# Turning softmax probabilities by a DMA transpose of sixteen-bit planes instead of by TensorE, in a hybrid attention block

## The reference, cut to what matters

```python
s = jnp.einsum('bcqhd,bckhd->bhcqk', qc, kb).astype(jnp.float32) * (Dh ** -0.5) + bias[None]
s = jnp.where(valid[None, None, :, None, :], s, -jnp.inf)
p = jax.nn.softmax(s, axis=-1).astype(v.dtype)
o = jnp.einsum('bhcqk,bckhd->bcqhd', p, vb)
...
ya = out_a.reshape(B, T, D_A) * jax.nn.silu(ga)
x = x + jnp.einsum('bte,ed->btd', y, w_out[l])
```

## Time and profile before

| | |
|---|---|
| median of 3 runs | 528.12 us (527.5 to 530.15) |
| profiled execution, span from first to last instruction | 526.3 us; the page gives no other time for it |
| PE busy | 517.4 us, 2912 matmuls |
| PEld busy | 453.4 us |
| DVE busy | 366.6 us |
| ACT busy | 273.4 us |
| POOL busy | 31.0 us |
| granted TensorE clock, mean | 0.998 of full speed |
| bytes by DMA | 102.53 MB, 195 GB/s in the mean |

### The profile page before, as it was taken

The page is one execution under the profiler, slowest core; times in us unless marked ns, Lnnn a source line. Parts: engine busy times, 40 slices in busy tenths (PEclk is TensorE's granted clock), DMA queues, the critical chain, the costliest instruction groups (busy, mean ns, idle before and its releaser), DMA issues.

```text
span 526.3 us, 8274 instructions
## 1 busy us (share of the span) xinstructions
PE 517.4 (98%) x2912; PEld 453.4 (86%) x2912; DVE 366.6 (70%) x552; ACT 273.4 (52%) x403; POOL 31.0 (6%) x47
## 2 busy tenths in 40 slices
PE   8999999999999999999999999999999999999994
PEld 6989999888888888888888888888888888888883
DVE  4799776675756787868666767586877887646454
ACT  4786555454444444445464737365555566434342
POOL 1000054040500000000000000000000000000000
PEclk9999999999999999999999999999999999999999
DMA  7975798766675566663755554645546775566614
GB/s 245 340 263 164 236 263 277 214 175 199 208 246 177 176 202 201 176 199 110 236 159 165 157 178 152 193 155 168 165 156 186 251 242 178 183 202 185 208 45 159
DMA packets 75356, 102.53 MB, mean 195 GB/s; under 512 B 5536, under 2 KB 63808, under 8 KB 75072
## 3 DMA queue, kind: packets, MB, share of 16 engines
q1 hardware_dynamic: 73744, 96.68, 58.1%
q0 software_dynamic: 1296, 5.01, 3.0%
q10 hardware_dynamic: 288, 0.46, 0.3%
HBM read 99.24 MB, written 2.11 MB: 193 GB/s over the span
## 4 chain that ended last, share of the span: by engine, by line
PE 97%; DMA 1%; DVE 0%; ACT 0%; issue 0%; DVEq 0%; POOLq 0%
PE acc L456 39%; PE acc L460 19%; PE acc L425 8%; PE acc L426 8%; PE acc L427 8%; PE acc L476 4%; PE acc L484 3%; PE aux L486 2%; DMA gain<-norm_gain 1%; PE aux L601 1%; PE aux L622 1%; PE aux L627 0%; PE aux L629 0%; PE aux L598 0%; PE aux L599 0%; PE aux L597 0%
## 5 line engine op out<-in xcount | busy, mean ns | idle before, releaser
L456 PE MATMUL acc<-acts,hi_slots 128*128 128x512 f32 (+1 forms) x896 | 276.9, 390 | 0.0
L984 DVE TENSOR_TENSOR lo_slots<-raw_slots,hi_slots 128x1024 fp32r<-128x1024 f32 x166 | 205.0, 1241 | 100.0 <-ACT hi_slots L690 99.1
L690 ACT ACTIVATE hi_slots<-raw_slots 128x1024 fp32r<-128x1024 f32 x166 | 175.1, 1057 | 149.3 <-PE acc L460 86.5
L460 PEld LDWEIGHTS acc<-acts,lo_slots 128*128 128x128 f32 x896 | 167.4, 188 | 34.0
L460 PE MATMUL acc<-acts,lo_slots 128*128 128x256 f32 (+1 forms) x896 | 174.2, 276 | 0.0
L456 PEld LDWEIGHTS acc<-acts,hi_slots 128*128 128x128 f32 x896 | 136.5, 189 | 0.1
L425 PE MATMUL acc<-hi_slots,acts 128*128 128x512 f32 x192 | 74.7, 389 | 0.0
L426 PE MATMUL acc<-lo_slots,acts 128*128 128x512 f32 x192 | 74.7, 389 | 0.0
L427 PE MATMUL acc<-hi_slots,acts 128*128 128x512 f32 x192 | 74.7, 389 | 0.0
L427 PEld LDWEIGHTS acc<-hi_slots,acts 128*128 128x128 f32 x192 | 36.0, 188 | 7.6
L425 PEld LDWEIGHTS acc<-hi_slots,acts 128*128 128x128 f32 x192 | 36.0, 188 | 7.5
(11 more groups left out here) (180 smaller groups left out, 458.1 us busy)
## 6 DMA issues: line engine op xcount, KB each, us to landing
raw_slots<-w_blocks SPq DMA_DIRECT2D x140, 512.0 KB, 4.2
raw_slots<-wo_blocks SPq DMA_DIRECT2D x32, 512.0 KB, 4.2
raw_slots<-w_blocks SPq DMA_DIRECT2D x8, 256.0 KB, 5.7
qk<-x POOLq DMA_DIRECT2D x1, 2048.0 KB, 10.2
qk<-xT SPq DMA_DIRECT2D x7, 256.0 KB, 6.6
o<-ext_dram POOLq DMA_DIRECT2D x1, 1024.0 KB, 8.1
fgain<-final_gain POOLq DMA_DIRECT2D x1, 1024.0 KB, 7.7
out<-o SPq DMA_DIRECT2D x2, 512.0 KB, 3.0
```

Source lines behind the costliest of these rows:

```text
L456: nc.tensor.matmul(whole, w_hi4[:, u % RING, q, f * HD:f * HD + HD], acts[:, k, :, tokens], start=(k == 0), stop=False)
L460: last = nc.tensor.matmul(acc[:, bank:bank + n], w_lo4[:, u % RING, q, f * HD:f * HD + HD], a_hi[:, k, tokens], start=False, stop=(k == KT ...
L690: nc.scalar.activation(hi_slots[:, s, 0:UK * CB], w_raw[:, s, :], ACT.Copy).then_inc(hi_done, 1)
L984: nc.vector.tensor_tensor(lo_slots[:, s, 0:UK * CB], w_raw[:, s, :], hi_slots[:, s, 0:UK * CB].bitcast(f32), ALU.subtract).then_inc(lo_don ...
```

## The change

The probabilities of a pair are put into one tensor `probs` (early and late side by side) and turned by one DMA. An f32 word is taken as two sixteen-bit halves. ACT copies the 768 words of a partition as 2 x 768 sixteen-bit integers into two planes (`planes_out`); SP issues one transposing DMA of the 12 blocks of 128x128 sixteen-bit elements, from SBUF to SBUF (`turn_planes`); ACT joins the turned planes to f32 words in `probs_T` (`pT_out`), and after that copies the high part pT_hi from there; DVE's low part is taken from there as well. The planes lie in `qiT`, which is free by then. The six transposes of PE and the two copies from PSUM to SBUF go; the semaphores of aux1 and aux2 that guarded them go too.

On SP the transpose of pair i stands in block i + 11 between the loads of units 1 and 2, behind a wait for the planes (for pair 7 between the loads of units 1 and 2 of the first output block). The value products of pair i move from block i + 10, before unit 7, to the next block, behind unit 0. `planes_out` stands on ACT behind the first features_low, pT_out behind stage_q, pT_rest behind DVE's stage_rest, `output` behind split 12, and for pair 7 output and gated move behind split 4 of the first output block.

```diff
+        probs_T = sb("probs_T", [P, 2, P + T])
+        probs = sb("probs", [P, 2, P + T])
+        p0, p1 = probs[:, :, 0:P], probs[:, :, P:P + T]
+        pT0, pT1 = probs_T[:, :, 0:T], probs_T[:, :, T:T + P]
...
+        WORDS = 2 * (P + T)
+        planes = flat(qiT[:, :, :]).bitcast(u16)[:, 0:2 * WORDS].rearrange("p (s n) -> p s n", s=2)
+        planes_T = flat(qiT[:, :, :]).bitcast(u16)[:, 2 * WORDS:4 * WORDS].rearrange("p (s n) -> p s n", s=2)
+
+        def halves(words):
+            return flat(words[:, :, :]).bitcast(u16).rearrange("p (n s) -> p s n", s=2)
...
+            def turn_planes(pair):
+                sp.wait_ge(planes_made, pair + 1)
+                sp.dma_start_transpose(flat(planes_T).rearrange("p (t q) -> p t q", q=P),
+                                       flat(planes)).then_inc(planes_turned, 16)
+
+            def feature_block(g, row, turned=None):
                 for u in range(UNITS):
+                    if u == 2 and turned is not None:
+                        turn_planes(turned)
                     sp.wait_ge(lo_done, g * UNITS + (u - RING + 1))
...
             def score_pair(pair, k_chunk):
...
-                pe.wait_ge(aux_read[1], pair + AUX1_PAIRS)
+                pe.wait_ge(aux_read[1], AUX1_PAIRS)
+                if pair > 0:
+                    pe.wait_ge(biased, pair)
...
             def value_pair(pair):
-                pe.wait_ge(aux_read[1], pair + (AUX1_PAIRS + 1))
-                pe.wait_ge(aux_read[2], pair + (AUX23_PAIRS + 1))
-                pe.wait_ge(aux_read[3], pair + AUX23_PAIRS)
+                pe.wait_ge(pt_lo_done, pair + 1)
+                pe.wait_ge(aux_read[3], pair + AUX3_PAIRS)
...
                 feature_unit(g, 0)
+                if pair > 0:
+                    value_pair(pair - 1)
                 feature_unit(g, 1)
...
-                feature_unit(g, 4)
-                feature_unit(g, 5)
-                transpose_pair(pair)
-                feature_unit(g, 6)
-                value_pair(pair)
-                feature_unit(g, 7)
+                for u in range(4, UNITS):
+                    feature_unit(g, u)
...
                 unit(G_OUT, u)
+                if u == 0:
+                    value_pair(HEADS - 1)
...
+            def planes_out(pair):
+
+                act.wait_ge(normed, pair + 1)
+                nc.scalar.activation(planes, halves(probs), ACT.Copy).then_inc(planes_made, 1)
+
             def pT_out(pair):
-                act.wait_ge(pt_done, pair + 1)
-                nc.scalar.activation(pT_hi, aux[2][:, :], ACT.Copy).then_inc(pt_hi_done, 1)
-                nc.scalar.activation(flat(pT1[:, :, :]), aux[1][:, 0:2 * P], ACT.Copy).then_inc(aux_read[1], 1)
+                act.wait_ge(planes_turned, 16 * pair + 16)
+                nc.scalar.activation(halves(probs_T), planes_T, ACT.Copy).then_inc(words_made, 1)
+                act.wait_ge(words_made, pair + 1)
+                nc.scalar.activation(pT_hi.rearrange("p (h t) -> p h t", h=2), pT0,
+                                     ACT.Copy).then_inc(pt_hi_done, 1)
...
                 features_low(g, 0, 0)
+                planes_out(i)
                 split_hi(g, 7)
                 split_hi(g, 8)
-                pT_out(i)
                 split_hi(g, 9)
                 stage_q(q_next, k_next, keys)
+                pT_out(i)
                 split_hi(g, 10)
-                output(i)
                 features_low(g, 1, 0)
                 split_hi(g, 11)
                 split_hi(g, 12)
+                output(i)
                 split_hi(g, 13)
...
             y_hi(1)
-            output(7)
             y_hi(2)
...
             split_hi(G_OUT, 4)
+            output(7)
             split_hi(G_OUT, 5)
...
             def pT_rest(pair):
                 dve.wait_ge(pt_hi_done, pair + 1)
-                nc.vector.tensor_tensor(pT_lo, aux[2][:, :], pT_hi.bitcast(f32),
-                                        ALU.subtract).then_inc(aux_read[2], 1)
+                hi, lo = (t.rearrange("p (h t) -> p h t", h=2) for t in (pT_hi, pT_lo))
+                nc.vector.tensor_tensor(lo, pT0, hi.bitcast(f32), ALU.subtract).then_inc(pt_lo_done, 1)
...
-            gated(3, 1)
             y_lo(6)
             split_lo(G_OUT, 4)
+            gated(3, 1)
             split_lo(G_OUT, 5)
```

More of the change, by code:

```diff
@@ L60, in hybrid_block @@
     f32r = mybir.dt.float32r
+    u16 = mybir.dt.uint16
     ALU = mybir.AluOpType
@@ L100, in hybrid_block @@
         low = sb("low", [P, 2, 2, T])
-        ki_bd = sb("ki_bd", [P, 2, T])
-        ki_nat = sb("ki_nat", [P, TM, P])
+        probs_T = sb("probs_T", [P, 2, P + T])
+        probs_T_flat = probs_T[:, :, :].rearrange("p h t -> p (h t)")
+        ki_bd = probs_T_flat[:, 0:2 * T].rearrange("p (h t) -> p h t", h=2)
+        ki_nat = probs_T_flat[:, 2 * T:3 * T].rearrange("p (m t) -> p m t", m=TM)
         w_idx1 = sb("w_idx1", [P, IDX_H])
@@ L123, in hybrid_block @@
         ones = sb("ones", [P, 1])
-        p1 = sb("p1", [P, 2, T])
-        p0 = sb("p0", [P, 2, P])
-        pT1 = sb("pT1", [P, 2, P])
+        probs = sb("probs", [P, 2, P + T])
+        p0, p1 = probs[:, :, 0:P], probs[:, :, P:P + T]
+        pT0, pT1 = probs_T[:, :, 0:T], probs_T[:, :, T:T + P]
         neg_max = sb("neg_max", [P, 2, 2])
@@ L221, in hybrid_block @@
         normed = sem("normed")
-        pt_done = sem("pt_done")
+        planes_made = sem("planes_made")
+        planes_turned = sem("planes_turned")
+        words_made = sem("words_made")
         pt_hi_done = sem("pt_hi_done")
+        pt_lo_done = sem("pt_lo_done")
         pv_done = sem("pv_done")
@@ L245, in hybrid_block @@
         AUX1_INDEX, AUX1_PAIRS = 1, 5
-        AUX23_PAIRS = 1
+        AUX3_PAIRS = 1
         HALF = CHUNK
@@ L354, in _, with out_unit @@
             token_block(G_VA, ROW_VA)
-            with sp.Fori(G_QKA, G_OUT) as g:
-                feature_block(g, g)
-            with sp.Fori(G_OUT, G_END) as g:
+            feature_block(G_QKA, G_QKA)
+            for g in range(G_QKA + 1, G_OUT):
+                feature_block(g, g, g - (G_QKA + 1))
+            def out_unit(g, u):
+                sp.wait_ge(lo_done, g * UNITS + (u - RING + 1))
+                load(u, wo_blocks[ds(g - G_OUT, 1), u, :, :].rearrange("o p c -> (o p) c"))
+            for u in range(2):
+                out_unit(G_OUT, u)
+            turn_planes(HEADS - 1)
+            for u in range(2, UNITS):
+                out_unit(G_OUT, u)
+            with sp.Fori(G_OUT + 1, G_END) as g:
                 for u in range(UNITS):
-                    sp.wait_ge(lo_done, g * UNITS + (u - RING + 1))
-                    load(u, wo_blocks[ds(g - G_OUT, 1), u, :, :].rearrange("o p c -> (o p) c"))
+                    out_unit(g, u)
             for n, (m, c) in enumerate(VECTOR_PARTS):
@@ L897, in gate_block @@
                 features_low(g, 0, 0)
+                planes_out(i + 4)
                 split_hi(g, 7)
@@ L900, in gate_block @@
                 split_hi(g, 8)
-                pT_out(i + 4)
                 split_hi(g, 9)
@@ L904, in gate_block @@
                     stage_q(q_next, q_next + 4, 8)
+                pT_out(i + 4)
                 split_hi(g, 10)
@@ L909, in _ @@
                 gate_block(g, i, i + 1)
-                output(i + 4)
                 features_low(g, 1, 0)
@@ L914, in _ @@
                 tanh_gate(i, 1)
+                output(i + 4)
                 split_hi(g, 13)
@@ L1353, in feature_attention @@
                 split_lo(g, 8)
-                pT_rest(i)
                 split_lo(g, 9)
                 stage_rest(q_next, k_next, i + 1)
+                pT_rest(i)
                 split_lo(g, 10)
@@ L1380, in gated @@
                 dve.wait_ge(gate_rated, 2 * i + (half + 1))
-                dve.wait_ge(aux_read[3], 2 * i + (half + AUX23_PAIRS + 1))
+                dve.wait_ge(aux_read[3], 2 * i + (half + AUX3_PAIRS + 1))
                 nc.vector.tensor_tensor(y, y, z[:, half, :], ALU.mult).then_inc(gate_step, 1)
@@ L1395, in gate_block @@
                 split_lo(g, 8)
-                pT_rest(i + 4)
                 split_lo(g, 9)
@@ L1399, in gate_block @@
                     stage_rest(i + 1, i + 5, i + 5)
+                pT_rest(i + 4)
                 split_lo(g, 10)
```

1 line of the change is left out of this document (removed).

## The result

| | before | after |
|---|---|---|
| median of 5 runs each | 528.37 us (527.5 to 530.15) | 524.25 us (524.02 to 525.87) |
| ratio | | 0.9936, 95% interval 0.9921 to 0.995 |
| span of the profiled execution | 526.3 us | 523.8 us |

The forecast was 524.5 us. The change takes 4.1 us off. The sum of the forecast came out right, but two of its terms were off in opposite directions, as the profile after shows.

What follows compares the result with a forecast made beforehand. PE, busy 98% of the 526.3 us span, was taken as the bound: less 5.3 us of transposes, plus a 1.7 us wait, plus 1.8 us from span to median gave 524.5 us; whole range 522.7 to 540.

Steps and rivals of the forecast that it cites:

- Removed, 5.3 us: 48 transposes leave PE in the attention blocks, 0.66 us for each of 8 pairs, a gain of at most 5.3 us.
- Added on ACT: Parting and joining passes at 1.5 us each, net 21 us in all on ACT, hidden if in time.
- D: Time from the planes being made to the transposing DMA's landing, taken as 5.5 us.
- Deadlines of pairs 0 to 6: PE waits before value products only if D exceeds 7.8 us, or 8.65 in pairs 4 to 6.
- Pair 7, wait of D - 3.8, at least 0.7: PE's wait for y_lo(0) before the first output unit, 1.7 us with D of 5.5.
- Sum: Span 526.3 - 5.3 + 1.7 = 522.7, plus 1.8 to reach the median: 524.5 us.
- B: Rival: DMA runs piece by piece, D is 9.1, PE waits at every value product: 534.7 us, chance 0.2.
- C: Rival: serial DMA stretches, D is 14.4, weights late too: 577.1 us, chance 0.1.
- A: Rival: gain eaten by D of 6.4 to 8.6, or half-rate ACT passes with D of 5: 526.2 us, chance 0.2.
- the formula: Span as 521.0 + (D - 3.8) + 4 (D - 7.8) + 3 (D - 8.65), positive brackets only, first at least 0.7.
- break-even: The D at which PE's waits cancel the whole gain, put at 8.1 us.
- The page against the change: Trainium skill page: 390 ns on TensorE against 1309 ns by DMA; twelve blocks in turn would make D 15.7 us.

Runs made afterwards that it cites:

- E1: Kernel after, with the six transposes of each pair put back on PE between units 5 and 6, into a bank nobody reads: 528.67 us, 1.0014 of before.
- E2: Kernel after, with pair 7's join and high and low parts moved behind y_hi(0), y_hi(1) on ACT and y_lo(0), y_lo(1) on DVE: 522.52 us, 0.9894 of before.
- E6: Kernel after, with the joining pass walking word by word, writing without a stride and reading the two planes in turn: 523.63 us, 0.9906 of before.
- E3: Kernel after, with the transpose done twice in series, the second issued when the first has landed: 533.69 us, 1.0104 of before.
- E8: Kernel after, with each pair's transpose issued as twelve DMAs of one 128x128 block each: 619.74 us, 95.5 us more than after.
- E4: Kernel after, with value products back in the pair's own block before unit 7: 552.9 us in the quicker two executions (1.0468 of before), 562.11 and 562.4 in the others.
- E5: Kernel after, with the transpose done three times in series, each issued when the one before has landed: 572.28 us.
- E7: Kernel after, with pair 7's join moved behind y_hi(0) and y_hi(1) and the joining pass walking word by word: 522.7 us, 0.9886 of before.

## Why the prediction was right, step by step

- **Removed, 5.3 us:** right. E1 takes 4.4 back, plus the 0.7 that the last wait absorbs; E2 shows 5.2 gained once nothing waits.
- **Added on ACT:** the parting pass was priced at 1.5 us and takes 1.47; the joining pass was priced the same and takes 1.94. Busy time grew by 23.7 us, not 21. The step "1.5 us each, because element count sets the f32 rows" failed for the joining pass; E6 shows that the order of its reads and writes is part of its price.
- **D, 5.5 us:** wrong by 1.75; it is 3.75. The count of pieces was right, 1,536 (and 32 packets more), but a quarter of the way towards 66 ns a piece was too much at 13 ns. Twelve blocks cost SP 1.44 us, not 4.4. The 4.2 us of a plain load, or the 3.6 of the 96 KB copy inside SBUF, would have been nearer.
- **Deadlines of pairs 0 to 6:** they hold in the kernel after, none is missed. The 7.8 us is 7.6 by the profile after for pair 2; E3 shows it by having only 0.2 us of waits in pairs 1 to 6 at D near 7.5. For pair 0 it is 5.4: I read pair 2's block and took it for all. Had D been 5.5 as forecast, pair 0 would already have been at its edge: that it was not is owed to the shorter D.
- **Pair 7, wait of D - 3.8, at least 0.7:** the place was right, and the floor applied, as D is under 4.5. With the join 0.45 us longer the floor is 1.15, and 1.2 was measured. 1.7 had been summed; the shorter D and the longer join partly cancel.
- **Sum:** 521.0 + 1.2 + 1.8 = 524.0 against 524.25. The 524.5 of the forecast had 0.5 us too much of a wait in it. The mechanism was right: PE's time is the kernel's, everything added is hidden but for one wait, at the first output unit. That the number is within 0.3 us is in part luck, as the D that was 1.75 too long and the join that was 0.45 too short pull opposite ways.
- **Rivals:** B and C, and A by its first condition, needed D above 6.4; it is 3.75. A's other condition, ACT's two passes at half the rate (3.0 us each) with D of 5, falls with passes of 1.47 and 1.94 us. The price of a late landing as a function of D was too low. E3, at D of 7.5 to 7.9, would have cost by the formula 521.0 + 4.1 + 1.8 = 526.9, and cost 533.7, slower than before. So break-even lies below the 8.1 us that I gave, between 3.75 and 7.5. The formula left out the clock that falls behind a long wait, and pair 0.
- **The page against the change:** the 1309 ns that the Trainium skill ("VectorE: DVE Perf Modes", The three transpose paths) gives for a block by DMA is close to what one instruction holds SP here, 1.23 us, and E8's landing 17.4 us behind the planes (246.56 to 263.99) is near the estimate of 15.7 from it. It is not the price of a block when twelve share an instruction: those land together in 3.7 us. The measurement decides: in this kernel, where PE is the bound, the transposes by DMA took 4.1 us less than those on TensorE.

## What to carry to other kernels

When an engine is the bound, moving its work to a path that takes several times as long can be a gain if the consumer can be placed after the landing (here 4.1 us with the products a block later, and a loss of 4.7% with them in the same block); find the deadline in each block, the first and the last above all, because that is where the cover differs. Put all blocks to be turned in one transposing DMA: here the instruction costs, not the block. Count a wait of the matmul engine at more than its length when it is some 2 us or longer: here 0.8 to 2.4 us more, as the clock falls behind it. What lies between 1.2 and 2.0 us was not tried.

## What the runs showed that was not expected

- **The clock behind a wait.** PE's granted clock stayed at 1.00 (2.4 GHz) over the wait of 1.2 us in the kernel after, and was at 0.50 (1.2 GHz) for some us behind waits of 2.0 us (E3, pair 0), 3.9 us (E4) and 4.8 us (E3, pair 7), with PE busy again at once. The same holds for each of the 26 waits of 2.0 us and more in the profiles of E3, E4, E5 and E8. The price beyond the waits themselves: 1.7 us each in E3, 2.1 in E5, in E8 95.5 - 76.5 = 19.0 us, 2.4 each, and in E4 2.0 in the profiled execution and some 0.8 in the quicker two.
- **A transposing DMA lands no later than a plain load of like size.** 384 KB from SBUF to SBUF, transposed, land in 3.7 us, where a 512 KB load from outside takes 4.4. Size and source differ, and no plain copy of 384 KB inside SBUF was run, so this does not say which of the two is quicker by itself.
- **The start of a run varies by more than some of the steps studied.** The first score stood at 234.1 to 236.6 us in the ten profiles, with the same instructions ahead of it. In the profile after, the first four matmuls of the weights took 2.08 us, in the profile before 1.25, both with the clock given as 1.00:

```profile
6.39 2.08 PE L506 MATMUL acc<-hi_slots,acts 128*128 128x512 f32 x4 [1.11 <-DVE acts L1056]
```

The two behind them start 0.43 us apart, as at 1.2 GHz in E3, although the clock is given as 1.00 here; whether it was really lower stays open. Comparing from a fixed point behind the start leaves this out: E2 and E7, alike there by theory, agree within 0.1 us.
